# Four of the six modulation parts moved out of the opening stage into the attention's first two groups

## What is computed

```
sil_c, sil_cc = silu(c), silu(c_ctx)
mx = sil_c @ w_ada + b_ada                 # 6 parts of 1024
mc = sil_cc @ w_ada + b_ada
xsh1, xsc1, xg1, xsh2, xsc2, xg2 = split(mx, 6)
px = split_in((x * (1 + xsc1) + xsh1) @ w_in)      # ctx likewise, with csh1, csc1
...  hgrn heads, conformer convolution, attention (8 heads in 4 groups)
x = layer_norm(ALPHA * x + xg1 * mix_x)
x = layer_norm(ALPHA * x + xg2 * peer(x * (1 + xsc2) + xsh2))
```

## Time and profile before

| | us |
|---|---|
| median of 3 runs | 4687.06 |
| lowest, highest | 4684.68, 4692.15 |
| the profiled execution | 4684.26 |
| its span in the trace | 4682.5 |
| modulation phase, of the span | 0 to 107 |
| mixers: input and heads | 107 to 690 |
| mixers: attention | 690 to 1073 |
| later phases | 1073 to 4682.5 |

### The profile page before, as it was taken

One profiled execution on the slowest core, in us unless ns is written; L12 is line 12 of the kernel. 1 busy time (PEld: TensorE's weight loads), 2 busy tenths in 40 slices (PEclk: granted clock), 3 DMA queues, 4 the chain that ended last, 5 costly groups with the idle time before them and its releaser, 6 DMA issues. The chain is left out here.

```text
span 4682.5 us, 54133 instructions
## 1 busy us (share of the span) xinstructions
PE 4333.3 (93%) x20787; PEld 3485.6 (74%) x20787; DVE 2632.3 (56%) x4621; ACT 1797.6 (38%) x2539; POOL 502.7 (11%) x308
## 2 busy tenths in 40 slices
PE   8988889878998988999999997999999999999998
PEld 6867766646874566999999985777788877787887
DVE  0777767783436897777777764344433333434332
ACT  1655655443421133433333324354332233633222
POOL 0000000000002601444444420000000000000000
PEclk9999999999999998999999998999999999999999
DMA  7111111103222246988888852212322321122322
GB/s 271 59 41 41 37 41 41 54 0 105 93 72 81 67 165 267 322 296 299 297 300 300 296 196 77 68 48 77 97 90 94 96 85 63 43 86 92 98 93 83
DMA packets 203058, 589.30 MB, mean 126 GB/s; under 512 B 18112, under 2 KB 73664, under 8 KB 201280
## 3 DMA queue, kind: packets, MB, share of 16 engines
q1 hardware_dynamic: 164944, 444.78, 28.5%
q0 software_dynamic: 36864, 134.23, 8.2%
q10 hardware_dynamic: 1008, 7.03, 0.4%
HBM read 553.99 MB, written 31.98 MB: 125 GB/s over the span
## 5 line engine op out<-in xcount | busy, mean ns | idle before, releaser
L404 DVE TENSOR_TENSOR tile_rest<-tile_raw,tile_up 128x1024 fp32r<-128x1024 f32 (+2 forms) x288 | 338.6, 1180 | 785.5 <-ACT tile_up L395 785.3
L412 PE MATMUL layer_psum<-hn_up,tile_up 128*128 128x512 f32 x1344 | 534.0, 397 | 21.2 <-DVE hn_rest L499 21.2
L413 PE MATMUL layer_psum<-hn_up,tile_rest 128*128 128x512 f32 x1344 | 526.9, 392 | 0.0
L414 PE MATMUL layer_psum<-hn_rest,tile_up 128*128 128x512 f32 x1344 | 526.6, 392 | 0.0
L395 ACT ACTIVATE tile_up<-tile_raw 128x1024 fp32r<-128x1024 f32 (+2 forms) x288 | 291.4, 1017 | 369.9 <-PE layer_psum L414 368.2
L412 PEld LDWEIGHTS layer_psum<-hn_up,tile_up 128*128 128x128 f32 x1344 | 255.2, 190 | 82.0 <-issue 29.7
L2316 PE MATMUL ex_psum<-ex_v_up,ex_prod_up 128*128 128x512 f32 x768 | 299.5, 390 | 1.9 <-DVE ex_prod_rest L2425 1.9
L2318 PE MATMUL ex_psum<-ex_v_rest,ex_prod_up 128*128 128x512 f32 x768 | 300.6, 391 | 0.0
L2320 PE MATMUL ex_psum<-ex_v_up,ex_prod_rest 128*128 128x512 f32 x768 | 300.5, 391 | 0.0
L413 PEld LDWEIGHTS layer_psum<-hn_up,tile_rest 128*128 128x128 f32 x1344 | 255.2, 190 | 53.9 <-issue 1.9
L414 PEld LDWEIGHTS layer_psum<-hn_rest,tile_up 128*128 128x128 f32 x1344 | 254.6, 189 | 54.1
(11 more groups left out here) (460 smaller groups left out, 10120.7 us busy)
## 6 DMA issues: line engine op xcount, KB each, us to landing
tT<-in_peer_v SPq DMA_DIRECT2D x128, 512.0 KB, 5.7
ex_u<-in_peer_u SPq DMA_DIRECT2D x104, 512.0 KB, 5.3
tile_raw<-in_w_gu SPq DMA_DIRECT2D x88, 512.0 KB, 3.4
xT<-in_w_head SPq DMA_DIRECT2D x56, 512.0 KB, 3.5
mod_w<-in_w_ada SPq DMA_DIRECT2D x48, 512.0 KB, 4.7
mg_w_raw<-in_w_merge SPq DMA_DIRECT2D x48, 512.0 KB, 3.5
expert_table<-et_rows SPq DMA_DIRECT2D x6, 4096.0 KB, 11.5
ex_rows<-expert_table SPq DMA_DIRECT2D x64, 384.0 KB, 7.0
```

What stands on the lines that cost most here:

```text
L404: self.nc.vector.tensor_tensor(out=self.rest[:, n % self.SLOTS, 0:blocks, :], in0=self.raw[n % self.RAWS][:, 0:blocks, :], in1=self.up[:, ...
L412: self.nc.tensor.matmul(dst, w_up, up, start=first, stop=False)
L413: self.nc.tensor.matmul(dst, w_rest, up, start=False, stop=False)
L414: return self.nc.tensor.matmul(dst, w_up, rest, start=False, stop=last)
```

## The change

The first phase makes only parts 0 and 1: its loops run twice, `rows` is a third as long, and 16 transposes are left. `sil` moves to memory that lives through the second phase.

The other 32 tiles are multiplied in the attention's groups 0 and 1. GpSimd, once the last head's `o_filled` is there, loads them one after another into four slots, which are blocks 4 and 5, 6 and 7 of `attT` and of `convT`; from the fifth on each load waits for the product of the tile four before. PE multiplies two or three tiles (`mod_of`) in each of fourteen places, the units 1 to 7 of group 0 and 0 to 6 of group 1: behind the wait for `turn_out` and ahead of the wait for `prob_ready`. Here the tile is the weight (128 x 128, eight times) and the two columns of `sil` move. The sums go to 64 columns in the second half of bank 1, already with channels on the partitions, so that no transposes are needed. At the end of the phase DVE adds the bias and the one of part 4, after a wait for all of the attention. FIRST_PARTS is 2. In the diff, the wait of `act` stands before ACT writes block 4 of `attT`, the first of `dve` before tap 0 of block 4 of `convT`, and the last piece at the end of DVE's work in the phase.

```
-            with sp.Fori(0, 6) as i:
+            with sp.Fori(0, FIRST_PARTS) as i:
...
-            for m in range(48):
+            for m in range(DB * FIRST_PARTS):
...
+        mod_slots = [tiles[:, b:b + 2, :].rearrange("p b t -> p (b t)").rearrange("p (d n) -> p d n", d=DB)
+                     for tiles in (mem.attT, mem.convT) for b in (4, 6)]
+        MOD_TILES = (6 - FIRST_PARTS) * DB
+        MOD_PLACES = 14
+        mod_sums = ph.whole[:, 512 + W - 512:512 + W - 512 + 2 * MOD_TILES]
+        def mod_of(i, u):
+            n = i * UNITS + u - 1
+            if not 0 <= n < MOD_PLACES:
+                return range(0)
+            return range(n * MOD_TILES // MOD_PLACES, (n + 1) * MOD_TILES // MOD_PLACES)
...
+        @block.gpsimd
+        def _(pool):
+            pool.wait_ge(o_filled, START + HEADS)
+            for m in range(MOD_TILES):
+                slot = m % len(mod_slots)
+                if m >= len(mod_slots):
+                    pool.wait_ge(mod_made, START + m - len(mod_slots) + 1)
+                pool.dma_start(mod_slots[slot], io["w_ada"][FIRST_PARTS + m // DB, m % DB]
+                               ).then_inc(mod_landed[slot], 16)
...
+                def modulation(m):
+                    slot = m % len(mod_slots)
+                    pe.wait_ge(mod_landed[slot], 16 * (m // len(mod_slots)) + 16)
+                    for d in range(DB):
+                        last = nc.tensor.matmul(mod_sums[:, 2 * m:2 * m + 2], mod_slots[slot][:, d, :], mem.sil[:, d, :],
+                                                start=d == 0, stop=d == DB - 1)
+                    last.then_inc(mod_made, 1)
...
                     pe.wait_ge(turn_out, START + i * TURNS + u + u // TB)
+                    for m in mod_of(i, u):
+                        modulation(m)
                     pe.wait_ge(prob_ready, START + i * UNITS + u + 1)
...
+                        if i * 2 + u // TB == DB // 2:
+                            act.wait_ge(mod_made, START + MOD_TILES)
...
+                        if h == DB // 2:
+                            dve.wait_ge(mod_made, START + MOD_TILES)
...
+            dve.wait_ge(turn_out, START + KV * TURNS)
+            dve.wait_ge(mod_made, START + MOD_TILES)
+            nc.vector.tensor_tensor(out=mem.mod[:, rest, :], in0=mod_sums.rearrange("p (m c) -> p m c", c=2), in1=bias,
+                                    op=ALU.add).then_inc(mod_out, 1)
+            dve.wait_ge(mod_out, START + 1)
+            nc.vector.tensor_scalar_add(mem.mod[:, 4 * DB:5 * DB, :], mem.mod[:, 4 * DB:5 * DB, :],
+                                        1.0).then_inc(mod_out, 1)
```

More of the change, by code:

```diff
@@ L37 @@
 T_DENSE = 3 * P
+FIRST_PARTS = 2
 EARLY = [(2 * k + 1) * NKEYS // 48 for k in range(24)]
@@ L629, in phase_modulation @@
     with Phase(nc, "mod") as ph:
-        w = ph.stream(8, [(6, 8, list(range(8)))])
+        w = ph.stream(8, [(FIRST_PARTS, 8, list(range(8)))])
         B = ph.banks()
-        cond, sil = ph.sb("cond", [P, DB, 2]), ph.sb("sil", [P, DB, 2])
+        cond, sil = ph.sb("cond", [P, DB, 2]), mem.sil
         masks = ph.sb("masks", [P, N_MASKS, P])
-        rows = ph.sb("rows", [2, 6 * D])
+        rows = ph.sb("rows", [2, FIRST_PARTS * D])
         x, cm = mem.attT, mem.convT[:, 0:4, :].rearrange("p b t -> p (b t)").rearrange("p (d c) -> p d c", c=C)
@@ L657, in _ @@
             nc.scalar.activation(sil[:], cond[:], ACT.Silu).then_inc(sil_ready, 1)
-            with act.Fori(0, 6) as i:
+            with act.Fori(0, FIRST_PARTS) as i:
                 for half in range(2):
@@ L666, in _ @@
             pe.wait_ge(sil_ready, START + 1)
-            with pe.Fori(0, 6) as i:
+            with pe.Fori(0, FIRST_PARTS) as i:
                 for k in range(8):
@@ L677, in _ @@
                     last.then_inc(w.filled, 1)
-            pe.wait_ge(row_out, START + CREDIT + 12)
+            pe.wait_ge(row_out, START + CREDIT + 2 * FIRST_PARTS)
             pe.wait_ge(x_loaded, START + 64)
-            for m in range(48):
+            for m in range(DB * FIRST_PARTS):
                 last = nc.tensor.transpose(B[2][:, 2 * m:2 * m + 2], rows[:, m * P:(m + 1) * P],
@@ L692, in _ @@
             dve.wait_ge(turned, START + 1)
[L693 to L698, removed]
+            n = DB * FIRST_PARTS
+            bias = mem.p("b_ada")[:, 0:n].unsqueeze(2).to_broadcast([P, n, 2])
+            seq(nc.vector.tensor_tensor(out=mem.mod[:, 0:n, :],
+                                        in0=B[2][:, 0:2 * n].rearrange("p (m c) -> p m c", c=2), in1=bias, op=ALU.add))
+            seq(nc.vector.tensor_scalar_add(mem.mod[:, DB:2 * DB, :], mem.mod[:, DB:2 * DB, :], 1.0))
             seq.end(1)
@@ L841, in phase_mixers @@
         c_made, c_up_ready, c_cut = sem("c_made"), sem("c_up_ready"), sem("c_cut")
+        mod_slots = [tiles[:, b:b + 2, :].rearrange("p b t -> p (b t)").rearrange("p (d n) -> p d n", d=DB)
+                     for tiles in (mem.attT, mem.convT) for b in (4, 6)]
+        mod_landed = [ph.sem_from_zero(f"mod_landed{n}") for n in range(len(mod_slots))]
+        mod_made, mod_out = sem("mod_made"), sem("mod_out")
+        MOD_TILES = (6 - FIRST_PARTS) * DB
+        MOD_PLACES = 14
+        mod_sums = ph.whole[:, 512 + W - 512:512 + W - 512 + 2 * MOD_TILES]
         ring.schedule(plan)
         block = ph.block()
+        def mod_of(i, u):
[3 more added lines that the diff above has]
+            return range(n * MOD_TILES // MOD_PLACES, (n + 1) * MOD_TILES // MOD_PLACES)
         N_HEADS = fills.number[("ca", 0)]
@@ L1504, in _ @@
             taps(HEADS * TAPS)
+            dve.wait_ge(turn_out, START + KV * TURNS)
+            dve.wait_ge(mod_made, START + MOD_TILES)
+            rest = slice(DB * FIRST_PARTS, 6 * DB)
+            bias = mem.p("b_ada")[:, rest].unsqueeze(2).to_broadcast([P, MOD_TILES, 2])
+            nc.vector.tensor_tensor(out=mem.mod[:, rest, :], in0=mod_sums.rearrange("p (m c) -> p m c", c=2), in1=bias,
[3 more added lines that the diff above has]
+                                        1.0).then_inc(mod_out, 1)
+            dve.wait_ge(mod_out, START + 2)
             dve.wait_ge(tapped, START + HEADS * TAPS)
@@ L3384, in build @@
                 mem.masks = sb("masks", [P, N_MASKS, P], U8)
+                mem.sil = sb("sil", [P, DB, 2])
                 phase_modulation(nc, io, mem)
```

## The result

The changed kernel takes 4708.12 us (median of 6 runs, 4700.09 to 4717.40) against 4687.24 for the kernel before in the same measurement (6 runs): a ratio of 1.0042, 95% interval 1.0031 to 1.0053. It is slower by 21 us; the forecast was slower by 26, 4713 us.

What follows compares the result with a forecast made beforehand. In the attention PE and DVE were taken as near balance at about 7.6 us a unit. Terms: -58.0 + 50.8 (59.2 - 8.4) + 0.6 = -6.6 us, plus 32 for the clock, about +26 on 4687.06: 4713 us, range 4675 to 4733.

Steps and rivals of the forecast that it cites:

- Removed, -58.0: First stage: four of six parts' tiles go, 55.9 us, and 32 of 48 transposes, 2.1 us; together 58.0 us less.
- Added on PE, +59.2: Attention groups 0 and 1: 512 more matmul records on PE at 116 ns each, 59.2 us more.
- Waits filled, -8.4: Fourteen places in groups 0 and 1: moved tiles fill all 8.4 us that PE waited before the transposes.
- Loads and queues, zero: Attention: GpSimd's 32 tile loads land in time and the added ACT and DVE waits cost nothing; zero.
- Rival D: Attention: GpSimd's loads land late and PE waits 3 us at each of seven refills; +14 us, 4701 us; chance 0.10.
- Tail, +0.6: End of the attention phase: DVE's two new operations and their waits are on the path, about 0.6 us more.
- The clock, +32: Groups 0 and 1: PE's clock falls to half in each of fourteen places, 2.3 us lost each; +32 us, bounds 22 and 43.
- Rival A: Groups 0 and 1: the clock holds at full rate; -6.6 us, 4680 us, or 4676 with 107 ns loads; chance 0.22.
- Rival C: Moved tiles on PE: cheap weight loads, 65 ns a record; -32.5 us, 4655 us; chance 0.12.
- a granted clock of 0.7 to 0.8: Groups 0 and 1: sign of the clock falling inside the places; staying above 0.95 would make the forecast wrong.
- not near 49: First stage: sign of the removal, last copy at about 44 us and the next stage starting near 49 us.
- DVE waiting: Fourteen places in groups 0 and 1: sign that PE is the late engine, its idle before the transposes near zero.

Runs made afterwards that it cites:

- e1: Changed kernel with the moved tiles' matmul operands swapped: two columns of sil are the weights, 128 columns move; 4685.12 us, ratio 0.9995 to the kernel before.
- e4: Changed kernel with only the first of eight matmuls done in each moved tile, all loads and waits kept; 4635.10 us, ratio 0.9890 to the kernel before.
- e7: Changed kernel with the 32 tiles dealt out to 28 spots of all four attention groups where PE had waited; 4654.61 us, ratio 0.9926 to the kernel before.
- e8: e7 with two of the three tiles at its first place put elsewhere; 4653.52 us, ratio 0.9927 to the kernel before.
- e3: Changed kernel with four parts kept in the first stage, so 16 tiles move, one or two in a place; 4685.75 us, ratio 0.9998 to the kernel before.
- e6: Changed kernel with every moved tile multiplied twice; 4819.55 us, ratio 1.0282 to the kernel before.

## Why the prediction was right

It was right in direction and in cause. That the total came within 5 us of the measured median is partly luck: two factors of the clock term were off in opposite ways. Its steps one by one, in its order.

*Removed, -58.0.* Measured -56.3 at the next stage's start. The start of the series was left as it was; the copies show that the series began 1.2 to 1.5 us later in this execution. By the first scores it is -55.0: a further 1.3 us were lost in the heads, with identical code there.

*Added on PE, +59.2.* The step took 116 ns a record and rejected the transposes (65 ns) as the wrong neighbour. The record cost 107 to 109 ns, so 512 x 0.109 = 55.8 us. The choice between the bounds was right, the value 3.4 us too high. What L1860's other 7 ns are, no run shows: it moves 128 columns, but so do e1's records, at 112 ns, and those of the old stage, at 109. That last figure was in the earlier trace rows and would have been the nearer neighbour. The Trainium skill's estimate in "TensorE: Matmul & The Clock Gate", section "LDWEIGHTS (loading the stationary operand)", 107 ns, was also nearer than 116; the trace agrees with it at full clock. That the load is what a record pays for isn't shown by that, since records with 2 weight columns take as long.

*Waits filled, -8.4.* Confirmed for the places, where none is left. A wait of 0.70 us in unit 7 of group 1 went too, so it is 9.2 us. With these terms the groups' growth at full clock would be 55.8 - 9.2 = 46.6 us; e1, which keeps the clock, has 49.8 with its longer records and 0.6 us more of waiting.

*Loads and queues, zero.* Confirmed by e4, and by the 3.9 and 3.8 us to landing where up to 10 were allowed. Rival D fell.

*Tail, +0.6.* The two DVE operations take 0.22 and 0.17 us, and the next phase's wait for PE's sequencer went from 3.12 to 3.67 us, 0.55 more:

```profile
1093.33 0.22 DVE L1547 TENSOR_TENSOR modulation<-mx_psum,params 128x64 f32<-128x64 f32 x1 [14.83 <-ACT attT L1277]
1093.59 0.17 DVE L1550 TENSOR_SCALAR modulation<-modulation 128x16 f32<-128x16 f32 x1
```

*The clock, +32.* Groups 0 and 1 grew by 76.3 us; less 46.6 that is 29.7 for the clock, and e1 against the changed kernel gives 26.5, or 28.0 if e1's records had cost 109 ns. The product was nearly right, but both factors were off, and in opposite ways, so its closeness is luck. The step was "I take a fall in each place: 14 x 2.3 = 32 us". There were 9 falls at places, with a mean of 6.8 us at half clock (61.3 us by the windows above without the one at 779.3), that is 3.4 us lost each: 9 x 3.4 = 31, of which a little lay beside waits. The prediction took the stay at half clock from stretches of other work (4.4, 3.25 and 6.1 us) and named what it left out, that tiles run on at half clock and make the stay longer. This is what happened in the three stays of over 10 us. That five places had no fall wasn't foreseen. They are all of two tiles, and the three longest stays are all at places of three; but what sets these five apart from the five places of two tiles that have a fall, I can't say from these traces: the one at 681.92 stands, as those with falls, between scores and transposes, and so does 705.61.

*Rival A*, that the clock holds, fell with 0.87 over groups 0 and 1, but its size was right: e1 is this rival made real, -6.1 us by the end of the attention where it said -6.6. The rule of the Trainium skill that was held for it ("TensorE: Matmul & The Clock Gate", section "HAM oscillation — how this bites in real kernels", against gaps of PE) did not decide here. PE was busy for the whole of the 7 us ahead of each of the nine falls at places; the window ahead of the one at 724.7, with its loader busy for 4.80:

```profile
717.70:724.70 7.00, 7.00 (x38) 4.80 (x37) 5.38 (x9) 2.30 (x4) 0.53 (x1) 1.00 0.00 0
```

*Rival C* would need 65 ns a record; it was 109.

The forecast on the spans was -6.6 + 32 = +25.4, and they differ by 23.3: +3.0 for the smaller removal, -3.4 for the records, -0.8 for the waits, -2.3 for the clock and +1.5 for groups 2 and 3 with the tail, to 0.1. The medians differ by 20.9, 2.4 us less than the two spans; single executions of one kernel differ by more than that.

One of the signs it named did not come: it wanted a granted clock of 0.7 to 0.8 over groups 0 and 1, and it was 0.87. The error lies in that sign and not in the sum, since 32 us lost are 64 us at half clock in some 256, which is a mean of about 0.87. The next stage started at 51.18 us and not near 49. The others came: no wait before the transposes in the places, DVE waiting, and the phases behind equal to 0.1 us.

## What to carry to other kernels

A moved piece of work has to be priced together with what it does to the clock of its neighbours: here the work's own balance was -6 to -8 us (e1 and the terms above), and the falls behind it cost 26 to 30. Before one moves work "into the waits", list the waits and count them: the fourteen places held 8.4 us of wait for 55.8 us of work, while the attention as a whole held 65, which e7 and e8 used for a gain of 34. And of two operand orders with the same time per matmul, the one that moves 128 columns and loads 2 kept the clock in this kernel.

## What the runs showed of the hardware that I had not expected

The granted clock fell to 0.50 in stretches where PE had no idle time at all. The clearest case is the place of unit 3 of group 1; windows of the changed kernel, before the fall, just ahead of it and behind it:

```profile
845.90:849.40 3.50, 3.50 (x33) 3.48 (x32) 3.18 (x6) 0.00 (x0) 0.53 (x1) 1.00 0.10 11
849.40:851.00 1.60, 1.60 (x17) 1.60 (x16) 1.53 (x3) 0.00 (x0) 0.53 (x1) 1.00 0.79 300
851.10:854.40 3.30, 3.30 (x18) 3.30 (x18) 1.53 (x3) 1.30 (x2) 0.53 (x1) 0.50 0.77 226
```

PE is busy for the whole of all three rows and its loader for 3.48 of 3.50 and 1.60 of 1.60 us, and the clock falls. With the operands swapped (e1) PE is as busy in the places, with as many records, and none of the fourteen has a fall. So the busy time of PE alone does not tell what the clock will do here. The operand order makes the difference at the same places, and so does how many such records stand close together: e3's twelve places of one tile and e8's units of groups 0 and 1 keep 1.00 with the order unchanged.

At half clock a record that moves only 2 columns takes twice as long too: 109 ns became 213. And e6 shows that the loss grows faster than the work: 512 such records cost 76.3 us as the change has them (waits filled included), the next 512 another 109.
